# Four seams into feed-forwards: residual sums transposed unweighted, norm gains applied out of PSUM, first high products of gate and up regrouped

## The reference

```python
for l in range(DEPTH):
    x = x + 0.5 * swiglu(rms_norm(x, ffn1_norm[l]), ffn1_w_gate[l], ffn1_w_up[l], ffn1_w_down[l])
    h = rms_norm(x, mix_norm[l]); ...; x = x + mixed @ w_out[l]
    x = x + 0.5 * swiglu(rms_norm(x, ffn2_norm[l]), ffn2_w_gate[l], ffn2_w_up[l], ffn2_w_down[l])
return rms_norm(x, final_norm)

def swiglu(h, w_gate, w_up, w_down):
    return (jax.nn.silu(h @ w_gate) * (h @ w_up)) @ w_down
```

## Time and profile before

| what | us |
|---|---|
| median of 3 runs | 1422.89 (1422.56 to 1425.86) |
| the profiled execution, its own time | 1426.32 |
| its span, first to last instruction | 1424.4 |
| PE busy | 1373.0 (96%) |
| PEld, DVE, ACT busy | 1185.6, 986.8, 780.4 |
| mean TensorE clock granted | 0.993 of full |

### The profile page before, as it was taken

One profiled execution on the slowest core, in us unless ns is written; L12 is line 12 of the kernel. 1 busy time (PEld: TensorE's weight loads), 2 busy tenths in 40 slices (PEclk: granted clock), 3 DMA queues, 4 the chain that ended last, 5 costly groups with the idle time before them and its releaser, 6 DMA issues.

```text
span 1424.4 us, 28209 instructions
## 1 busy us (share of the span) xinstructions
PE 1373.0 (96%) x10866; PEld 1185.6 (83%) x10866; DVE 986.8 (69%) x1543; ACT 780.4 (55%) x1296; POOL 9.4 (1%) x23
## 2 busy tenths in 40 slices
PE   7998999999999999999999999999999999999997
PEld 7986887878888889877888887888879987888886
DVE  6977627877666677657766667766677856876665
ACT  6455547766545566435655546555565633655454
POOL 0000000000000000000000000000000000000000
PEclk9999999999999999999999999999999999999999
DMA  8732453245555554203565555556545401465561
GB/s 295 292 123 74 163 212 128 74 150 204 180 193 193 188 177 149 89 4 107 194 205 190 177 194 172 200 192 199 181 152 195 141 19 50 168 215 178 190 200 51
DMA packets 62789, 229.82 MB, mean 161 GB/s; under 512 B 7008, under 2 KB 7264, under 8 KB 62448
## 3 DMA queue, kind: packets, MB, share of 16 engines
q1 hardware_dynamic: 60912, 220.23, 46.0%
q0 software_dynamic: 1792, 8.37, 1.6%
HBM read 227.53 MB, written 1.05 MB: 160 GB/s over the span
## 4 chain that ended last, share of the span: by engine, by line
PE 89%; DVE 6%; ACT 3%; issue 1%; DMA 0%; DVEq 0%; SPq 0%; ACTq 0%
PE PS L793 24%; PE PS L1113 23%; PE PS L1133 16%; PE PS L1115 11%; PE PS L782 1%; PE PS L772 1%; PE PS L1325 1%; PE PS L1319 1%; DVE x_res L1959 1%; DVE out_operands L2055 1%; PE PS L871 1%; DVE w_lo L2033 1%; PE PS L1287 1%; PE PS L859 1%; PE PS L897 1%
## 5 line engine op out<-in xcount | busy, mean ns | idle before, releaser
L1113 PE MATMUL PS<-hT_both,w_hi 128*128 128x512 f32 x1376 | 489.7, 398 | 0.0
L1115 PE MATMUL PS<-hT_both,w_lo 128*128 128x256 f32 x1376 | 386.2, 281 | 0.0
L1113 PEld LDWEIGHTS PS<-hT_both,w_hi 128*128 128x128 f32 x1376 | 258.6, 188 | 62.9
L1115 PEld LDWEIGHTS PS<-hT_both,w_lo 128*128 128x128 f32 x1376 | 259.9, 189 | 3.1
L793 PE MATMUL PS<-hT_both,w_hi 128*128 128x256 f32 x1392 | 255.6, 286 | 2.3 <-DVE w_lo L2033 1.2
L793 PEld LDWEIGHTS PS<-hT_both,w_hi 128*128 128x128 f32 x1392 | 217.8, 192 | 6.6 <-issue 5.2
L2315 DVE TENSOR_TENSOR w_lo<-weight_ring,w_hi 128x1024 fp32r<-128x1024 f32 x176 | 207.1, 1218 | 2.4 <-ACT w_hi L1736 2.4
L793 PE MATMUL PS<-hT_both,w_lo 128*128 128x256 f32 x696 | 197.1, 283 | 0.0
L2321 DVE TENSOR_TENSOR w_lo<-weight_ring,w_hi 128x1024 fp32r<-128x1024 f32 x88 | 107.8, 1225 | 110.4 <-ACT w_hi L1745 110.4
L1736 ACT ACTIVATE w_hi<-weight_ring 128x1024 fp32r<-128x1024 f32 x176 | 175.4, 1045 | 0.0
L2033 DVE TENSOR_TENSOR w_lo<-weight_ring,w_hi 128x1024 fp32r<-128x1024 f32 x107 | 125.8, 1219 | 47.7 <-ACT w_hi L1514 47.4
(11 more groups left out here) (309 smaller groups left out, 1824.0 us busy)
## 6 DMA issues: line engine op xcount, KB each, us to landing
weight_ring<-in_stream SPq DMA_DIRECT2D x411, 512.0 KB, 4.4
norm_gain<-in_gains_in POOLq DMA_DIRECT2D x8, 512.0 KB, 4.1
consts<-in_csts POOLq DMA_DIRECT2D x1, 1864.0 KB, 9.9
arena<-in_taps_in SPq DMA_DIRECT2D x4, 384.0 KB, 3.5
arena<-in_bias_in POOLq DMA_DIRECT2D x1, 1152.0 KB, 12.5
x_res<-in_x_in SPq DMA_DIRECT2D x2, 512.0 KB, 3.8
lora<-in_lora_in POOLq DMA_DIRECT2D x2, 512.0 KB, 3.6
x_out<-yT SPq DMA_DIRECT2D x2, 512.0 KB, 2.7
```

The lines of the kernel that those rows point to most:

```text
L1113: pe.matmul(PS[:, b, :], Wh[:, u, k, :], HT2[:, k], start=(k == 0), stop=(k == KT - 1), skip_group_check=True)
L1115: ins = pe.matmul(PS[:, b, 0:T], Wl[:, u, k, :], Hh[:, k, :], start=False, stop=(k == KT - 1), skip_group_check=True)
```

## The change

Only seams into late phases change in work. In the diff, `high_parts` and `low_parts` replace `high_first`.

```diff
 PAR: + ("norm_w", 6 * KT) ahead of conv_w; parameters() fills it with the gains of phases 2 to 7, by columns
-        ARENA = 35072
+        ARENA = 35048
@@ POOL
-                pool.wait_ge(sem("xn_made"), 4 * n)
+                pool.wait_ge(sem("xn_made"), 4 * early_before(n))
...
-                gain(n)
+                if not late(n):
+                    gain(n)
@@ PE, transposes_in
-                        pe.wait_ge(sem("xn_made"), 4 * n + 2 * t + half + 1)
+                        if late(n):
+                            pe.wait_ge(sem("x_made"), x_made_at(n - 1) + 2 * t + half + 1)
+                        else:
+                            pe.wait_ge(sem("xn_made"), 4 * early_before(n) + 2 * t + half + 1)
...
-                                               XG[:, t, kk * P:(kk + 1) * P], ident)
+                                               (X if late(n) else XG)[:, t, kk * P:(kk + 1) * P], ident)
@@ PE
+            def high_parts(n, u, near, clear=True, wait=True):
                 for i, w in enumerate((Wh, Wl)):
                     for k in range(KT):
+                        if wait and i == 0 and k in (0, KT // 2):
+                            if late(n):
+                                pe.wait_ge(sem("hT_by_act"), by_act_at(n) + (1 if k == 0 else 2))
+                                pe.wait_ge(sem("hT_by_dve"), by_dve_at(n) + (1 if k == 0 else 2))
...
+            def low_parts(n, u, far):
+                pe.wait_ge(sem("hT_by_dve"), by_dve_at(n + 1))
@@ PE, ffn, gate_up
+                    for part in range(2) if i == 0 else ():
+                        pe.wait_ge(sem("gu_lo"), 2 * f0 + part + 1)
+                        high_parts(n, part, PS[:, 4 + part, 0:T], True, part == 0)
                     for part in range(2):
...
-                        first = i == 0 and part == 0
-                        if first:
-                            ins = high_first(n, u, PS[:, b, 0:T], PS[:, b, T:2 * T])
-                        for k in () if first else range(KT):
+                        if i == 0:
+                            ins = low_parts(n, u, PS[:, b, T:2 * T])
+                        for k in () if i == 0 else range(KT):
@@ ACT
+            def weighted_high(n):
+                for i in range(2):
+                    act.wait_ge(sem("xT_made"), 4 * n + i + 1)
+                    for k in range(4):
+                        ins = act.activation(Hh[:, 4 * i + k, 0:P], PS[:, turned_bank(n) + i, k * P:(k + 1) * P],
+                                             ACT.Copy, scale=par("norm_w", KT * (n - 2) + 4 * i + k, 1))
+                    ins.then_inc(sem("hT_by_act"), 1)
...
-                    late_root(n, 0)
-                    hT_split(n)
-                    late_root(n, 1)
+                    squared = late_square(n, 0)
+                    weighted_high(n)
+                    late_root(0, squared)
+                    late_root(1, late_square(n, 1))
@@ DVE
-            def weighted(n, t, half):
...
+            def weighted_inputs(n):
+                for i in (2, 3):
+                    half = slice(4 * (i - 2), 4 * (i - 2) + 4)
+                    dve.wait_ge(sem("xT_made"), 4 * n + i + 1)
+                    dve.tensor_tensor(Hh[:, half, P:T], PS[:, turned_bank(n) + i, :].rearrange("p (k t) -> p k t", k=4),
+                                      bc(par("norm_w", KT * (n - 2) + 4 * (i - 2), 4), P), ALU.mult)\
+                       .then_inc(sem("hT_by_dve"), 1)
+                for i in range(4):
+                    cols = slice((i // 2) * P, (i // 2 + 1) * P)
+                    if i < 2:
+                        dve.wait_ge(sem("hT_by_act"), by_act_at(n) + i + 1)
+                    else:
+                        dve.wait_ge(sem("hT_by_dve"), by_dve_at(n) + i - 1)
+                    for k in range(4):
+                        kk = 4 * (i % 2) + k
+                        ins = dve.scalar_tensor_tensor(Hl[:, kk, cols], PS[:, turned_bank(n) + i, k * P:(k + 1) * P],
+                                                       par("norm_w", KT * (n - 2) + kk, 1), Hh[:, kk, cols],
+                                                       ALU.mult, ALU.subtract)
+                    ins.then_inc(sem("hT_by_dve"), 1)
@@ DVE, seam
                 if late(n):
                     for t in range(NTT):
-                        for half in range(2):
-                            added_to_x(n - 1, t, (half,))
-                            weighted(n, t, half)
-                else:
-                    inputs_normed(n)
+                        added_to_x(n - 1, t)
+                    weighted_inputs(n)
+                    roots_spread(n)
+                    return
+                inputs_normed(n)
```

More of the change, by code:

```diff
@@ L253, in parameters @@
     dup = lambda v: np.concatenate([v, v])[:, None]
+    put("norm_w", np.stack([col(g) for g in norm_gains(x)[2:-1]], 1))
     put("conv_w", x["a_conv_w"][0].reshape(CONV, 4, P).transpose(2, 0, 1))
@@ L640, in roots_at, with early_before, by_act_at, by_dve_at @@
             return sum(2 if late(m) else 4 for m in range(n))
+        def early_before(n):
+            return sum(not late(m) for m in range(n))
+        def by_act_at(n):
+            return sum(2 if late(m) else 4 for m in range(n))
+        def by_dve_at(n):
+            return sum(6 if late(m) else 4 for m in range(n))
         def late_before(n):
@@ L815, in job @@
                 if tt is None:
+                    both_first = n == 0 and late(phase)
+                    for i in range(tiles) if both_first else ():
+                        is_split(i + 1)
+                        high_parts(phase, q + i, PS[:, b, i * T:(i + 1) * T], i == 0, i == 0)
                     for i in range(tiles) if only is None else (only,):
@@ L819, in job @@
                         o = PS[:, b, i * T:(i + 1) * T]
-                        if n == 0 and i == 0:
-                            ins = high_first(phase, u, o, o)
+                        if n == 0 and i == 0 and not both_first:
+                            high_parts(phase, u, o)
+                        if both_first or n == 0 and i == 0:
+                            ins = low_parts(phase, u, o)
                             continue
@@ L1487, in rstd, with late_square, late_root @@
                        .then_inc(sem("rstd_made"), 1)
-            def late_root(n, t):
+            def late_square(n, t):
                 act.wait_ge(sem("x_made"), x_made_at(n - 1) + 2 * t + 2)
-                done.wait(done(act.activation(squares, X[:, t, :], ACT.Square, accum_out=stat[:, t:t + 1])))
+                return done(act.activation(squares, X[:, t, :], ACT.Square, accum_out=stat[:, t:t + 1]))
+            def late_root(t, squared):
+                done.wait(squared)
                 done.wait(done(act.activation(stat[:, 6 + t:7 + t], stat[:, t:t + 1], ACT.Ln,
@@ L1960, in added_to_x @@
                                              ALU.mult, ALU.add).then_inc(sem("x_made"), 1)
-            def weighted(n, t, half):
-                if t == half == 0:
-                    dve.wait_ge(sem("gain_loaded"), 16 * n)
-                cols = slice(half * 512, (half + 1) * 512)
-                dve.wait_ge(sem("x_made"), x_made_at(n - 1) + 2 * t + half + 1)
-                dve.tensor_tensor(XG[:, t, cols], X[:, t, cols], G[:, cols], ALU.mult).then_inc(sem("xn_made"), 1)
+            def weighted_inputs(n):
[9 more added lines that the diff above has]
+                        dve.wait_ge(sem("hT_by_act"), by_act_at(n) + i + 1)
+                    else:
+                        dve.wait_ge(sem("hT_by_dve"), by_dve_at(n) + i - 1)
[5 more added lines that the diff above has]
+                    ins.then_inc(sem("hT_by_dve"), 1)
             def roots_spread(n):
@@ L1985, in normed @@
                 if n:
-                    dve.wait_ge(sem("gain_loaded"), 16 * n)
+                    dve.wait_ge(sem("gain_loaded"), 16 * early_before(n))
                 else:
@@ L2018, in seam @@
                     half, cols = slice(4 * (i % 2), 4 * (i % 2) + 4), slice((i // 2) * P, (i // 2 + 1) * P)
-                    dve.wait_ge(sem("hT_hi"), 4 * n + i + 1)
+                    dve.wait_ge(sem("hT_by_act"), by_act_at(n) + i + 1)
                     dve.tensor_tensor(Hl[:, half, cols], PS[:, turned_bank(n) + i, :].rearrange("p (k t) -> p k t", k=4),
-                                      Hh[:, half, cols], ALU.subtract).then_inc(sem("hT_lo"), 1)
-                if late(n):
-                    roots_spread(n)
+                                      Hh[:, half, cols], ALU.subtract).then_inc(sem("hT_by_dve"), 1)
             now = {}
@@ L2584, in _ @@
                     ahead(n + 1)
[L2585 removed]
+            dve.wait_ge(sem("gain_loaded"), 16 * early_before(len(PHASES)))
             for t in range(NTT):
```

12 lines of the change are left out of this document (4 added, 8 removed).

## The result

The changed kernel takes 1430.22 us (median of 20 runs, 1423.47 to 1432.32) against 1425.4 (20 runs, 1421.8 to 1429.04) for the kernel before, on the same chip: ratio 1.0025, 95% interval 1.0015 to 1.0034. By the ratio it is slower by about 3.6 us (the medians lie 4.8 apart), where I had said 0.8 us less. Repeats gave 1.0028 (1.0016 to 1.004) and 1.001 (0.9994 to 1.0025). The profiled execution has a span of 1429.2 us (own time 1431.02), 4.8 over that of before.

A forecast was written before the change was run, and what follows sets the result against it. PE, 89% of the chain, was taken as the bound. Three seams at +0.19, one at -1.46 and 0.1 for parameters gave -0.8 us; less the profiled execution's excess over the median, 1422.1 us, range 1419.4 to 1427.2.

The forecast's parts named there:

- Type A: Three seams after output projections, last product to root row: +0.19 us each, the head's gain eaten by DVE's low parts.
- DVE's spacing: Seam's foot: sixteen 128x128 low-part operations on DVE start 0.26 us apart; each 0.01 of spacing is 0.6 us in all.
- The stall at the foot: PE's new wait for DVE's low parts ahead of its low products: 0.64 us in seams after output projections.
- low products: PE's sixteen products with the low parts at the seam's end: 2.02 us plus 0.16 for the last duration's end.
- ACT's eight copies: ACT makes the high parts of quarters 1 and 2 in eight 128x128 copies, 0.29 us each, 2.3 in all.
- Type B: The one seam after a feed-forward: earlier transpositions bring the root row to 877.92 from 879.38, -1.46 us.
- quarters start at 868.59: Seam after a feed-forward: PE turns the sums at once, starting quarters at 868.59, 869.07, 869.55 and 870.03, done at 870.70.
- The cover: Activation's low part for down of tile 0, delayed by DVE's queue: margin falls from 1.3 to 0.6 us, priced at nothing.
- the row: Trace row L2453, same DVE operation and size: 0.344 us long, last two 0.26 apart, used to price the sixteen.
- The count is no cost: PE's gate and up products in the seam: three of 0.12 us replace a 512 and a 256 together 0.354.
- my rivals: PE bound -3.2 (0.08); DVE serial +4.2 (0.05); slower (0.06); DVE queue late +3.2 (0.05); more won, some 5 (0.04).
- slower: Rival: DVE's sixteen low operations start 0.44 us apart like a dependent pair, +10 in all, 1432.9 us; chance 0.06.

The follow-up runs named there:

- new_spread: Changed kernel plus 111 and 86 empty PE increments, at most one behind each long product, both mixers at block position 28: 1425.17 us, ratio 0.9984 to the kernel before.
- after_third: The changed kernel unaltered, measured again on the same chip as the padded kernels: 1428.82 us, ratio 1.001 to the kernel before.
- old_spread: Kernel before plus 130 and 126 empty PE increments, placed singly under long products, both mixers at block position 28: 1423.82 us, ratio 0.9984.
- the first set: Here its repeat of the unaltered changed kernel against the kernel before: 1431.45 us, ratio 1.0028; at equal clock 1428.1 against 1426.4.

## Why the prediction was wrong

**The seams were right.** Type A: forecast +0.19, measured +0.08 by the chain; all four together: forecast -0.89, measured -0.98. DVE's spacing, the heart of the sum, was 0.26: sixteen in 4.22 with 0.343 each give (4.22 - 0.34)/15 = 0.258. The stall at the foot is 0.55, forecast 0.64; low products 2.15, forecast 2.18; ACT's eight copies 2.17, forecast 2.3 (0.38 long each, about 0.26 apart). The tenth too much came in ahead of DVE's weighting, which began 1.35 after the last product's end, not 1.52.

Type B: forecast -1.46, measured -1.23. The transpositions did not begin 0.15 before the last product's end but 0.15 behind it (870.99 against 870.84); from there the steps kept their distances. The step of the seams that failed is "quarters start at 868.59". The trace of before had the measure for it, in a row that I didn't use: there too the first transposition stood 0.15 behind the last product's end, 868.89 against 868.74.

L1133's successor for tile 0 (L1164) starts 5.83 after the root row and waits for nothing, with the activation's low part done 0.8 ahead, forecast 0.6. The cover held.

The formula of the Trainium skill that I set beside the row (VectorE: DVE Perf Modes, "The TRN2 errata — SBUF-src ops pay a fixed extra latency per instruction") gives, as an estimate, 0.29 for an operation of 128 elements; 0.258 was measured, so the row was the better price. That formula is for a tensor_tensor, and I had taken the wrong one: the table of the same section has 120 + FD cycles at 0.96 GHz for an operation out of PSUM (FD is its elements), an estimate of 0.258 for 128, and with that the trace agrees. (For its sixteen I wrote that the root row comes 0.45 later; 4.65 against my own 4.24 is 0.41.) The other rule that I took from the Trainium skill (VectorE: DVE Perf Modes, "The DRAIN you can't avoid"), that the next operation waits for an empty pipe, is not what these sixteen did: 0.258 apart at 0.343 long. The same section says that an operation that isn't held starts earlier, which I had left out, and with that the trace agrees.

**The step that failed** is the confinement itself: "the change touches only what lies between the last accumulator of a phase and the root row of the next", with "The count is no cost" for PE's products. I counted products within the seam and took their number for free, and of the instructions, 79 more in PE's program, I said nothing. The stream is a resource with edges of its own: a pause of PE ends when a block of 256 instructions has come in, and the 19 and 59 instructions more ahead of the mixers put these pauses elsewhere among the small products. The runs showed it by pads alone: with the change in place and 197 pads, new_spread ran 4.2 us under after_third. None of my rivals is the one that occurred; "slower" had its place in DVE's spacing, which was as forecast. The view of before had the clue, which I read past: an "issue" of 1.26 in the middle of 122 equal products.

**A second term was off, the base.** I took 1422.89 from three runs; over 20 runs the kernel before has 1425.4. So 2.5 of the 8.1 us between my 1422.1 and the measured 1430.22 were there before any change.

**What it costs.** At equal layout the change is worth between -1.3 (stretches) and -0.1 +/- 1 (runs). The layout costs after_third 4.2 against new_spread, and the kernel before 2.1 against old_spread, because before had one mixer at the good position already. The difference of 2.1, and the change's own -0.1, make the changed kernel's +2.0 in that set. In the first set it was +1.7 at equal clock. The +4.5 of the two profiles overstates it: against the mean stretches of their positions the kernel before was 0.9 short in its second mixer. The changed kernel's first 20 runs come to 1427.9 at equal clock, 1.1 to 1.8 over what the kernel before has in the four sets. So of the +3.6 of the first measurement I estimate 1.1 to 1.8 as the layout's less the change's own gain. The rest would be the clock of those runs; that of the kernel before in them is not on record, and nothing here shows that the change lowers it.

**What stays open.** Why a pause at a given edge takes 0.5 in one execution and 1.5 in the next is answered only in part: it ends 1.20 to 1.59 us behind the end of a transfer, and transfers take 0.9 to 1.5 us and don't always begin at the same product; what sets their beginning I haven't found. The drops of the granted clock were not steered, and why they change places is not explained.

## What to carry to other kernels

Count an engine's instructions, not only its busy time: where short instructions run densely (here 64x64 products at 0.015 us each), TensorE can stop once in every 256 instructions, for 0.5 to 1.8 us, and any edit ahead of it moves the stop. So an edit worth 1 us is to be judged by stretches of the trace between equal landmarks, and against a kernel padded to the same layout; a change in an untouched stretch is the sign. Pads go one at a time under long products, where they cost nothing; on an idle engine they cost 0.15 us each.

## What the hardware showed that I had not expected

- TensorE pauses at places 256 instructions apart in its stream, until 1.20 to 1.59 us after the end of a transfer of 16,384 bytes of instructions, as shown above. The Trainium skill (Runtime: NRT & Kernel Launch, "Instruction fetch mechanics") says that the refill comes in blocks of 16 KiB, which agrees with the page of the profile (64 transfers, 1.05 MB), and that crossing a boundary is mostly hidden. That holds in the feed-forwards, whose stretches repeat to 0.02 us from run to run, and it doesn't where 128 products with their weight loads take some 2 us.
- A semaphore increment on TensorE costs 0.153 us when nothing is in flight (20.12 to 13.40 us of idle for 130 to 86 of them), nothing when it stands alone behind a 512-column product, or some behind one of 256 (feed-forward 181.74 with 111 or none), and 0.012 to 0.014 with two on either side of the product (86 instructions for 1.00 us, 111 for 1.52).
- Sixteen DVE operations of 128x128 that don't read one another run 0.258 apart at 0.343 each, reading a PSUM bank and writing beside each other.
